# A diffusion trunk block: the first in-projection panel runs over feature chunks outermost, and the second panel uses the other weight slot

## The reference: what is computed

```python
zx = modulate(rms_norm(x, norm1_g[l]), mx[0], mx[1])
zc = modulate(rms_norm(h, norm1_g[l]), mc[0], mc[1])
rq, rk, rv, rg, aq, ak, av, cu, cv = split_in(zx @ w_in[l])        # w_in: 1024 x 2304
crq, crk, crv, crg, caq, cak, cav, ccu, ccv = split_in(zc @ w_in[l])
...                                    # retention, window attention, chunk gating on these
x = x + mx[2] * (concat(ret_x, att_x, cm_x) @ w_out[l])
x = x + mx[5] * swiglu(modulate(rms_norm(x, norm2_g[l]), mx[3], mx[4]), w_gate[l], w_up[l], w_down[l])
...                                    # the same for h in the first block
```

## Time and profile before

| | us |
|---|---|
| median of 3 runs | 1891.16 (1888.81 to 1891.89) |
| span of the profiled execution, first to last instruction | 1884.1 |
| TensorE busy in it | 1662.6 (88%) |
| VectorE, ScalarE, GpSimd busy | 699.9, 541.2, 516.5 |
| mean granted TensorE clock | 0.935 of full |

### The profile page before, as it was taken

One profiled execution on the slowest core, in us unless ns is written; L12 is line 12 of the kernel. 1 busy time (PEld: TensorE's weight loads), 2 busy tenths in 40 slices (PEclk: granted clock), 3 DMA queues, 4 the chain that ended last, 5 costly groups with the idle time before them and its releaser, 6 DMA issues.

```text
span 1884.1 us, 22935 instructions
## 1 busy us (share of the span) xinstructions
PE 1662.6 (88%) x9310; PEld 1343.1 (71%) x9310; DVE 699.9 (37%) x1108; ACT 541.2 (29%) x849; POOL 516.5 (27%) x231
## 2 busy tenths in 40 slices
PE   4789994688989999999999997996679799999998
PEld 2467774456877888888888886776447677778786
DVE  3442234663432322332223353516554422423324
ACT  3212222662252111111111125322652522222223
POOL 0712222001214322322323211333103253444431
PEclk8789997889989999999999998998799889999998
DMA  6434630000234232123332110221001224133221
GB/s 246 160 134 134 168 116 7 1 1 1 67 111 157 92 109 87 59 100 111 111 111 96 60 45 21 69 67 45 1 1 36 98 67 134 67 101 100 67 89 45
DMA packets 122192, 155.20 MB, mean 82 GB/s; under 512 B 20352, under 2 KB 89872, under 8 KB 122128
## 3 DMA queue, kind: packets, MB, share of 16 engines
q1 hardware_dynamic: 122128, 154.32, 25.3%
HBM read 152.21 MB, written 2.10 MB: 82 GB/s over the span
## 4 chain that ended last, share of the span: by engine, by line
PE 77%; DVE 11%; ACT 5%; issue 3%; SPq 2%; POOL 2%; DMA 2%; DVEq 0%; ACTq 0%; POOLq 0%
PE ps L1505 16%; PE ps L1506 15%; PE ps L1507 15%; PE ps L1801 5%; PE ps L1803 5%; PE ps L1802 5%; PE ps L1428 2%; PE ps L1687 2%; PE ps L1709 2%; DVE s_at L1274 1%; DVE hl L1367 1%; PE ps L1725 1%; PE ps L1820 1%; PE ps L1821 1%; PE ps L1822 1%
## 5 line engine op out<-in xcount | busy, mean ns | idle before, releaser
L1505 PE MATMUL ps<-zh,wh 128*128 128x512 f32 x1632 | 588.9, 361 | 32.8 <-POOL zl L445 11.2
L445 POOL TENSOR_TENSOR wl<-raw,wh 128x1024 fp32r<-128x1024 f32 x144 | 353.6, 2468 | 853.2 <-ACT wh L547 853.2
L1506 PE MATMUL ps<-zl,wh 128*128 128x512 f32 x1632 | 583.8, 358 | 0.0
L1507 PE MATMUL ps<-zh,wl 128*128 128x512 f32 x1632 | 580.0, 355 | 0.0
L1505 PEld LDWEIGHTS ps<-zh,wh 128*128 128x128 f32 x1632 | 312.2, 191 | 116.4 <-issue 42.8
L1507 PEld LDWEIGHTS ps<-zh,wl 128*128 128x128 f32 x1632 | 311.2, 191 | 45.9
L1506 PEld LDWEIGHTS ps<-zl,wh 128*128 128x128 f32 x1632 | 312.2, 191 | 42.6
L547 ACT ACTIVATE wh<-raw 128x1024 fp32r<-128x1024 f32 x144 | 148.5, 1058 | 398.3 <-PE ps L1507 280.5
L1380 DVE SCALAR_TENSOR_TENSOR xT<-ps,modcol,xT 128x512 f32<-128x512 f32 (+1 forms) x264 | 169.4, 661 | 103.8 <-PE ps L1803 100.3
L1361 DVE TENSOR_TENSOR hf<-gs,ps 128x512 f32<-128x512 f32 x66 | 37.5, 596 | 408.8 <-ACT gs L859 408.6
L1801 PE MATMUL ps<-hh,wh_d 128*128 128x512 f32 x480 | 174.0, 363 | 13.3 <-DVE xT L1380 13.2
(11 more groups left out here) (226 smaller groups left out, 1603.0 us busy)
## 6 DMA issues: line engine op xcount, KB each, us to landing
raw<-in_w_gate_dram SPq DMA_DIRECT2D x22, 1024.0 KB, 7.0
raw<-in_w_up_dram SPq DMA_DIRECT2D x22, 1024.0 KB, 9.4
raw_m<-in_w_mod_dram SPq DMA_DIRECT2D x22, 1024.0 KB, 5.1
raw_d<-in_w_down_dram SPq DMA_DIRECT2D x20, 1024.0 KB, 4.9
raw<-in_w_in_dram SPq DMA_DIRECT2D x14, 1024.0 KB, 5.4
raw<-in_w_mod_dram SPq DMA_DIRECT2D x11, 1024.0 KB, 5.2
raw_n<-in_w_mod_dram SPq DMA_DIRECT2D x9, 1024.0 KB, 5.2
raw<-in_w_out_dram SPq DMA_DIRECT2D x32, 256.0 KB, 4.4
```

What stands on the lines that cost most here:

```text
L445: nc.gpsimd.tensor_tensor(dst, src, hi.bitcast(F32), ALU.subtract).then_inc(sem(done), 1)
L1505: MM(dst, wt_h[:, h, w], zh[:, k, c0:c1], start=(k == 0), stop=False)
L1506: MM(dst, wt_h[:, h, w], zl[:, k, c0:c1], start=False, stop=False)
L1507: last = MM(dst, wt_l[:, h, w], zh[:, k, c0:c1], start=False, stop=(k == KC - 1))
```

## The change

Four edits belong together.

- TensorE: a new `first_panel` takes the place of `in_step(0)` in both blocks. It waits until both halves of panel 0 have their `wl`, and then goes over the chunks: wait for chunk k, six matmuls of half 0, six of half 1. The four accumulations (two halves, two column ranges) are in the banks 0 to 3 that they had before. In the first block the two `mod_half` of panel 0 come after it.
- TensorE: panels 1 and 2 are unrolled; panel 1 reads slot 1.
- ScalarE: the high parts of panel 1 go into slot 1, in the first block right after the norm's high parts, in the second before `norm_z` and after a wait for the last down matmuls of the first block (which read slot 1). After the halves of panel 0 ScalarE only moves the results out.
- GpSimd: the remainders of panel 1 go into slot 1, from the place that they had in its order.

```diff
-            def lo_a(a, h):
+            def lo_a(a, h, slot=0):
                 pool.wait_ge(sem("hiA"), 2 * a + h + 1)
-                lo(slot_half(wl[0], h), raw_half(panel_raw(a), h), slot_half(wh[0], h), "loA")
+                lo(slot_half(wl[slot], h), raw_half(panel_raw(a), h), slot_half(wh[slot], h), "loA")
...
             first_norm()
-            with pool.Fori(1, NP_IN + 1) as a:
+            lo_a(1, 0, slot=1)
+            lo_a(1, 1, slot=1)
+            with pool.Fori(2, NP_IN + 1) as a:
...
                     for a in range(A_IN[l] + 1, A_OUT[l] + 1):
-                        lo_a(a, 0)
-                        lo_a(a, 1)
+                        lo_a(a, 0, slot=int(a == A_IN[l] + 1))
+                        lo_a(a, 1, slot=int(a == A_IN[l] + 1))
...
                     first_norm_hi()
+                    for h in range(2):
+                        hi_a(1, h, "ld_in0", ld[2], first=True, slot=1)
                 else:
+                    act.wait_ge(sem("dn0_mm0"), KC * FSTEPS)
+                    act.wait_ge(sem("dn1_mm0"), KC * FSTEPS)
+                    for h in range(2):
+                        hi_a(A_IN[l] + 1, h, *PANEL_AT[A_IN[l] + 1][1:], first=True, slot=1)
                     norm_z(2, NT)
...
                         act.wait_ge(sem("use_a"), 2 * (a0 + p) + h + 1)
-                        if l == 0 and p + 1 < NP_IN:
+                        if p == 0:
+                            pass
+                        elif l == 0 and p + 1 < NP_IN:
                             hi_a(a0 + p + 1, h, "ld_in0", ld[p + 2])
...
+            def first_panel(a, norm_u):
+
+                pe.wait_ge(sem("loA"), 2 * a + 2)
+                for k in range(KC):
+                    z_wait(pe, norm_u, k)
+                    for h in range(2):
+                        w_h, w_l = wh[0][:, h, P * k:P * k + P], wl[0][:, h, P * k:P * k + P]
+                        for c0, c1, s in parts(True):
+                            dst = ps[:, h, :] if s == 0 else ps[:, h + 2, 0:SC]
+                            MM(dst, w_h, zh[:, k, c0:c1], start=(k == 0), stop=False)
+                            MM(dst, w_h, zl[:, k, c0:c1], start=False, stop=False)
+                            last = MM(dst, w_l, zh[:, k, c0:c1], start=False, stop=(k == KC - 1))
+                        if k == KC - 1:
+                            last.then_inc(sem("use_a"), 1)
...
-                in_step(0, True, first=True)
-                with pe.Fori(1, NP_CTX) as p:
+                first_panel(A_IN[l], 2 * l)
+                if l == 0:
+                    mod_half(0, raw[1], 1, 2)
+                    mod_half(1, raw_n, 5, 1)
+                in_step(1, True, slot=1)
+                for p in range(2, NP_CTX):
                     in_step(p, True)
                 in_step(NP_CTX, l == 0)
```

More of the change, by code:

```diff
@@ L553, in slot_half, with hi_a @@
                 return t[:, h, :].rearrange("p (k n) -> p k n", k=KC)
-            def hi_a(a, h, loaded, value, first=False):
+            def hi_a(a, h, loaded, value, first=False, slot=0):
                 act.wait_ge(sem(loaded), value)
@@ L560, in hi_a @@
                     act.wait_ge(sem("use_a"), 2 * a + h - 1)
-                copy(slot_half(wh[0], h), raw_half(panel_raw(a), h)).then_inc(sem("hiA"), 1)
+                copy(slot_half(wh[slot], h), raw_half(panel_raw(a), h)).then_inc(sem("hiA"), 1)
             def hi_b(l, s, h):
@@ L1495, in _, with three_pass @@
             mod_finish(3)
-            def three_pass(wt_h, wt_l, h, dsts, ctx, norm_u=None):
+            def three_pass(wt_h, wt_l, h, dsts, ctx):
                 for k in range(KC):
                     w = slice(P * k, P * k + P)
-                    if norm_u is not None:
-                        z_wait(pe, norm_u, k)
                     for c0, c1, s in parts(ctx):
@@ L1508, in three_pass, with panel_half @@
                 return last
-            def panel_half(a, h, ctx, norm_u=None):
+            def panel_half(a, h, ctx, slot=0):
                 pe.wait_ge(sem("loA"), 2 * a + h + 1)
-                three_pass(wh[0], wl[0], h, (ps[:, h, :], ps[:, h + 2, 0:SC]), ctx, norm_u).then_inc(sem("use_a"), 1)
+                three_pass(wh[slot], wl[slot], h, (ps[:, h, :], ps[:, h + 2, 0:SC]), ctx).then_inc(sem("use_a"), 1)
+            def first_panel(a, norm_u):
[11 more added lines that the diff above has]
+                            last.then_inc(sem("use_a"), 1)
             for l in range(DEPTH):
@@ L1517, in _, with in_step @@
                     norm(2 * l, NT)
-                def in_step(p, ctx, first=False):
+                def in_step(p, ctx, slot=0):
                     for h in range(2):
-                        if not first:
-                            pe.wait_ge(sem(f"ev_in{l}"), 2 * p + h - 1)
-                        panel_half(A_IN[l] + p, h, ctx, 2 * l if first and h == 0 else None)
+                        pe.wait_ge(sem(f"ev_in{l}"), 2 * p + h - 1)
+                        panel_half(A_IN[l] + p, h, ctx, slot)
                         if l == 0:
-                            if h == 0 and not first:
+                            if h == 0:
                                 mod_finish(J_IN + p - 1)
                             mod_half(h, (raw[1], raw_n)[h], (1, 5)[h], p + 2 - h)
-                in_step(0, True, first=True)
-                with pe.Fori(1, NP_CTX) as p:
+                first_panel(A_IN[l], 2 * l)
[4 more added lines that the diff above has]
+                for p in range(2, NP_CTX):
                     in_step(p, True)
```

## The result

| | before | after |
|---|---|---|
| median of four runs each, taken together | 1889.99 us (1884.86 to 1891.89) | **1874.95 us** (1869.96 to 1876.74) |
| ratio of the two | | 0.9917 (0.9897 to 0.9937) |
| span of the profiled execution | 1884.1 us | 1873.0 us |
| TensorE busy in it | 1662.6 us | 1659.1 us |

The kernel is faster, by 15 us. The forecast was 1878.1, its range 1875.0 to 1884.0: the time lies 3.2 us under the forecast and just under the range.

What follows compares the result with a forecast made beforehand. The prediction took TensorE, its work and the stalls between, to bound the kernel. 6.2 us in the first block plus 6.9 in the second made 13.1, so the median 1891.2 became 1878.1 us, range 1875.0 to 1884.0.

Steps and rivals of the forecast that it cites:

- What bounds it: TensorE bounds the kernel, with 77% of the span; panel 0's first half waits for `zl`, 5.5 and 8.2 us.
- The unit and the rise of the clock: Panel 0: 16 units of six matmuls, 1.96 us each until the clock rises at 4.85 us, then 1.05; 19.05 us.
- The rival with the old instants: Panel 0, both blocks: clock rises at 73.1 and 1151.9 as before, gains 5.0 and 5.2 us, time 1881.0; chance 0.20.
- First block, 6.2 us: Panel 0 starts 2.15 us later and takes 19.05 us; panel 1 starts at 86.7 instead of 92.89, gaining 6.2 us.
- The chunks don't hold it: First block's panel 0: the last `zl` is there at 81.0, the last two units begin only at 82.6.
- the wait keeps its length and the gain passes through it: First block: TensorE's 8.4 us wait for `modrow` moves with TensorE, so it takes nothing from the gain.
- Second block, 6.9 us: Panel 0 starts at 1143.14 as before; panel 1 starts at 1162.3 instead of 1169.36, 7.0 us, taken as 6.9.
- The loads: First block: panel 2's load lands at about 98, needed by about 102.7; cost 0, at worst 2.0 us.
- Everything else ... so 0: Panel 2 on, unrolled instead of looped, has the same instructions and TensorE's matmuls run on at 1.05 us per unit: 0.
- the swallowed block: First block's gain lost to panel 2's load or the `modrow` wait; only 6.9 us stay, 1884.3 us; chance 0.07.
- No effect: Panel 1 isn't ready in slot 1 when panel 0 ends, TensorE waits out the gain; about 1890 us; chance 0.05.
- slower: Second block: panel 1's load lands late, ScalarE's copies delay `norm_z`; a landing at 1160 gives about 1901; chance 0.03.

Runs made afterwards that it cites:

- the slot alone: Kernel before with panel 1's parts in slot 1 and panels 1 and 2 unrolled, old order of panel 0 in both blocks: 1889.09 us, ratio 0.9992.
- The warm start: Changed kernel with matmuls that belong to no result on TensorE ahead of panel 0, five in the first block, three in the second: 1874.98 us, ratio 0.9921.
- the early start: Changed kernel, but panel 0 starts at its first half's weights and waits for the second half's at their first use: 1873.13 us, ratio 0.9907.
- the second block alone: Changed kernel with the first block put back to the old order and panel 1 there to slot 0: 1881.21 us, ratio 0.9951.
- the kernels of one block each: Changed kernel with old order and slot 0 put back in the other block: first block alone 1882.02 us, second block alone 1881.21 us.
- the three further executions of before: Kernel before, no edit, profiled three more times: 1890.6, 1891.5 and 1889.6 us.

## Why the prediction was right or wrong, step by step

**What bounds it: right.** TensorE's waits inside panel 0, 5.5 and 8.2 - 4.7 = 3.5 us, are gone, its slow stretch is shorter, and nothing else in the first profile got shorter; the slot alone gives nothing.

**The unit and the rise of the clock: right in the mean.** 4.85 us after the start was taken, from the FFN's two restarts. In the changed kernel the clock rose after 3.3 and 5.4 us, and in its five other executions after 3.2 to 4.1 and 4.6 to 5.4. The rival with the old instants falls: its 5.0 and 5.2 us are not what the panels gave. In the second block it mattered less than the prediction's own ends (14.0 or 12.2 us in all) allow for. Its last `zl` ends at 1155.73; with the 0.15 for the signal and two units that is 1157.98, against an end at about 1158.4: TensorE's own work sets the end, but only 0.4 us above what the chunks allow. The warm start got back just these 0.4.

**First block, 6.2 us: too low by 0.4 after two opposite errors.** Start 2.11 us later (2.15 foretold), panel 0 to panel 1 9.10 us shorter: 7.0 us. Panel 0 took 18.4 us instead of 19.05, because the clock rose 1.5 us sooner than taken. "The chunks don't hold it" looked at the last chunk alone; the sixth, with three chunks' work behind it, leaves no room, and that is why the early start gained nothing. But the step "the wait keeps its length and the gain passes through it" was off by 0.4: the wait for `modrow` is 8.83 us in every execution with panel 1 in slot 1 in this block, the slot alone among them, and with it in slot 0 8.44, but once (the second block alone) 8.64. What of the slot does it wasn't followed up. That leaves 6.6.

**Second block, 6.9 us: right.** 26.22 - 19.41 = 6.8, and TensorE stood for no copy and no move. ScalarE's cover of 2.3 us measured 2.45 us, and GpSimd was done 1.2 us before the first `zl`. The Trainium skill (SBUF — State Buffer, "SBUF: two separate sides") has a VectorE instruction with two SBUF inputs block for the whole of a GpSimd instruction that reads SBUF. This case's traces agree: the first block's first `zl` starts at 62.28, GpSimd's instruction runs on to 60.58 + 2.35 = 62.93, and the `zl` takes 1.46 us; the second block's, after GpSimd's end, takes 0.96 for the same 768 columns. The first block's two rows:

```profile
62.28 1.46 DVE L1049 TENSOR_TENSOR zl<-nxz_s,zh 128x768 fp32r<-128x768 f32 x1 [2.00 <-ACT zh L549]
60.58 2.35 POOL L445 TENSOR_TENSOR wl<-raw,wh 128x1024 fp32r<-128x1024 f32 x1 [2.38 <-ACT wh L549]
```

**The loads: right.** Panel 2's load was told to land at about 98 and to cost 0; it was there at 97.2.

**"Everything else ... so 0", and the level: wrong.** These are the steps that failed; the terms of the two panels were right. By the landmarks the overlap is 6.6 + 6.8 = 13.4 us, against 13.1, while the kernel gained 15.0 us in the first comparison and 16.8 over all executions.

First, the level: the sum was taken from a median of three runs, 1891.16, where 57 executions give 1890.1, which is 1.1 us. Second, the spread: the text took the 7.1 us between span and median for time outside the span. That time is 1.8 us, and the other 5.3 were the spread of this kernel, which lay in the prediction's own numbers. Its range allowed 1.5 us for that spread, while the 57 executions of before lie between 1883.9 and 1896.4. With 1890.1 and 13.4 the forecast would have been 1876.7.

Third, the 0 for everything else: in the means the kernel gains 3.4 us more than the overlap (16.8 - 13.4). Of it 0.4 times 3.6 us = 1.4 us is the clock that stays up at the `vtok` waits, if the four in ten are its true share and the old order's share is nil; that the new order causes it isn't shown. The cause of the other 2 us stays open; the interval of the difference alone is 1.4 us to either side, so they may be none.

**The rivals and the chances.** No effect and slower fell with the first profile, the swallowed block with the kernels of one block each. "Faster by over 0.2%", at 0.92, is what came.

## What to carry to other kernels

A panel that waits for its input chunk by chunk should do all it can with a chunk before it asks for the next; the gain is the idle time in it, until its end is some late chunk plus the work on it and on those behind it. Then neither an earlier start nor a higher clock buys anything. That chunk needn't be the last: here, in the first block, it was the sixth of eight, because the last three came faster than they were used. Such an order needs the next panel's weights ready elsewhere at its end: here the second slot, worth nothing by itself, kept waits of 0.9 and 2.7 us away. Before a forecast is put on a median, the profiled execution's own time (span plus the same margin outside it in every run) is to be compared with the runs: a difference is the kernel's spread, and belongs into the range.

## What the runs showed of the hardware

With gaps in its work TensorE's clock rose later. In panel 0 of the old order in the second block a chunk's six matmuls, 1.96 us at the low level, came every 2.39 us, and the granted clock rose 8.7 to 8.9 us after the first matmul in all six executions. With the new order, and no gaps, it rose after 4.3 to 5.4 us in all nine without added matmuls. In the first block the old order has 10.0 to 12.7 us (TensorE busy for 9.78 of the first 12.40 in the first of the three further executions of before), the new one, where both halves' weights were waited for, 3.2 to 4.1. The Trainium skill (TensorE: Matmul & The Clock Gate, "What's actually happening") says that the moment of the rise varies from run to run with where the first matmul falls; the spread within each group agrees. The distance between the groups is the work's: in seven of the nine the panel began 8.2 to 8.5 us after the clock's last fall, as in the six with the old order, and the clock still rose 3.4 us sooner.

The same waits of 1.9, 1.05 and 1.26 us within 6 us brought the clock down in twelve of sixteen executions and left it up in four, and that is worth 3.6 us each time. The distance between the extreme executions of one kernel, 9.3 and 12.6 us here, holds several such cases: the first block has two more stretches with two lengths (39.6 or 40.4 to 40.8, 63.8 or 65.4 us).

A VectorE subtraction of 128x768 in float32 took 0.96 us with GpSimd idle and 1.46 us when it started 0.65 us before the end of a GpSimd instruction.
